# Layer two's up projection, steps one to eight: four quarters over the whole depth become seven half-block products

## The reference, cut to what matters

```python
D_MODEL, SEQ, D_FF, CONV_W = 1024, 512, 2816, 3

def conv_ffn(h, w_up, conv_w, conv_b, w_down):
    S = h.shape[1]
    u = h @ w_up                                  # [512, 1024] @ [1024, 5632]
    up = jnp.pad(u, ((0, 0), (CONV_W - 1, 0), (0, 0)))
    u = conv_b + sum(conv_w[j] * up[:, j:j + S] for j in range(CONV_W))
    gate, val = jnp.split(u, 2, axis=-1)
    return (jax.nn.silu(gate) * val) @ w_down

for layer in range(2):
    x = x + mixer(rms_norm(x, norm_mix[layer]))
    x = x + conv_ffn(rms_norm(x, norm_ffn[layer]), f_w_up[layer], ...)
```

## Time and profile before

| | us |
|---|---|
| median of 3 runs | 1189.49 |
| lowest, highest | 1187.22, 1190.43 |
| the profiled execution, whole | 1190.18 |
| its span | 1188.4 |
| PE busy | 1174.7 (99%) |
| DVE busy | 865.1 (73%) |
| ACT busy | 616.4 (52%) |
| POOL busy | 353.1 (30%) |
| DMA queues' share: SP's, POOL's | 31.2%, 16.3% |
| TensorE's mean granted clock | 0.998 |

### The profile page before, as it was taken

How to read it: one execution, slowest core, us unless ns; L and a number is a source line. 1 busy time by engine, 2 the same in 40 slices (tenths; PEclk the granted TensorE clock), 3 DMA queues, 4 the chain that set the end, 5 groups by cost and what they waited for, 6 DMA issues and landing times.

```text
span 1188.4 us, 18961 instructions
## 1 busy us (share of the span) xinstructions
PE 1174.7 (99%) x6874; PEld 999.3 (84%) x6874; DVE 865.1 (73%) x1502; ACT 616.4 (52%) x1033; POOL 353.1 (30%) x429
## 2 busy tenths in 40 slices
PE   9999999999999999999999999999999999999998
PEld 7768886778888888889999887988888888889998
DVE  6588968945766666579897888855766666579986
ACT  6554337854534333345566789945534334345563
POOL 0633547830042432211000367730042421211000
PEclk9999999999999999999999999999999999999999
DMA  7555352253398785436544110053377574325553
GB/s 277 185 183 204 142 198 69 73 142 106 106 232 243 197 211 194 173 111 212 186 160 138 62 37 2 1 125 107 106 190 182 150 177 132 106 71 196 188 173 127
DMA packets 51555, 174.54 MB, mean 147 GB/s; under 512 B 4720, under 2 KB 6128, under 8 KB 41504
## 3 DMA queue, kind: packets, MB, share of 16 engines
q1 hardware_dynamic: 36352, 127.51, 31.2%
q0 software_dynamic: 15136, 46.14, 16.3%
HBM read 171.50 MB, written 52.47 MB: 188 GB/s over the span
## 4 chain that ended last, share of the span: by engine, by line
PE 92%; DVE 4%; ACT 1%; DMA 1%; issue 1%; POOL 0%; SPq 0%; DVEq 0%; ACTq 0%
PE ps L2558 27%; PE ps L2560 27%; PE ps L2559 27%; PE ps L2273 3%; PE ps L2257 3%; PE ps L2073 1%; PE ps L2524 1%; DMA raw<-w_sums 1%; PE ps L2114 1%; DVE w_lo L1705 1%; PE ps L2144 1%; PE ps L2241 1%; ACT probs L977 1%; DVE xT L1725 0%; PE ps L2081 0%
## 5 line engine op out<-in xcount | busy, mean ns | idle before, releaser
L2558 PE MATMUL ps<-h_hi,w_hi 128*128 128x512 f32 x704 | 274.5, 390 | 0.0
L2560 PE MATMUL ps<-h_hi,w_lo 128*128 128x512 f32 x704 | 273.9, 389 | 0.0
L2559 PE MATMUL ps<-h_lo,w_hi 128*128 128x512 f32 x704 | 273.9, 389 | 0.0
L1394 DVE TENSOR_TENSOR w_lo<-raw,w_hi 128x2048 fp32r<-128x2048 f32 (+1 forms) x62 | 123.0, 1984 | 118.3 <-ACT w_hi L887 118.3
L1216 ACT ACTIVATE cv<-u_in,vec 128x512 f32<-128x512 f32 x88 | 71.2, 816 | 178.8 <-DVE u_in L1835 176.7
L887 ACT ACTIVATE w_hi<-raw 128x2048 fp32r<-128x2048 f32 (+1 forms) x72 | 121.8, 1692 | 69.1 <-PE ps L2560 69.1
L2558 PEld LDWEIGHTS ps<-h_hi,w_hi 128*128 128x128 f32 x704 | 132.2, 188 | 27.8 <-issue 0.7
L2560 PEld LDWEIGHTS ps<-h_hi,w_lo 128*128 128x128 f32 x704 | 132.2, 188 | 27.5
L2559 PEld LDWEIGHTS ps<-h_lo,w_hi 128*128 128x128 f32 x704 | 132.2, 188 | 27.3
L762 POOL TENSOR_TENSOR v<-act 128x256 f32<-128x256 f32 x16 | 43.3, 2709 | 345.2 <-DVE act L1876 345.2
L2558 PE MATMUL ps<-a_hi,w_hi 128*128 128x256 f32 (+1 forms) x440 | 139.0, 316 | 0.8 <-DVE a_lo L1709 0.8
(11 more groups left out here) (276 smaller groups left out, 2426.6 us busy)
## 6 DMA issues: line engine op xcount, KB each, us to landing
raw<-in_f_up SPq DMA_DIRECT2D x44, 1024.0 KB, 5.0
w_sums<-in_f_w_down POOLq DMA_DIRECT2D x22, 1024.0 KB, 8.7
w_sums<-in_f_w_down POOLq DMA_DIRECT2D x44, 512.0 KB, 8.8
raw<-w_sums SPq DMA_DIRECT2D x44, 512.0 KB, 4.1
raw<-in_a_in_wide SPq DMA_DIRECT2D x12, 1024.0 KB, 6.1
raw<-in_f_w_down SPq DMA_DIRECT2D x22, 512.0 KB, 3.9
raw<-in_f_w_down SPq DMA_DIRECT2D x22, 256.0 KB, 3.9
bias_tiles<-bias_rows SPq DMA_DIRECT2D x1, 4096.0 KB, 26.2
```

The source lines that it names most:

```text
L1394: dve.tensor_tensor(w_lo[:, s, 0:n], raw[:, s, 0:n], w_hi[:, s, 0:n].bitcast(F32), ALU.subtract)\
L2558: pe.matmul(dst, s_hi, m_hi, start=start, stop=False)
L2559: pe.matmul(dst, s_hi, m_lo, start=False, stop=False)
L2560: return pe.matmul(dst, s_lo, m_hi, start=False, stop=stop)
```

## The change

Layer one stays as it was in what it computes. In layer two's up projection, steps 1 to 8 are computed by seven products: the step's four channel tiles (gate pair, value pair), the depth (features 0 to 511, 512 to 1023) and the tokens (0 to 255, 256 to 511) are each halved. One product is 2 channel tiles x 4 feature tiles x 3 matmuls of 256 columns, 24 matmuls; a step has 168. ACT copies four intermediate PSUM results out (`keep`), DVE combines them. Before step 1 ACT makes eight gained copies of the features, DVE four sums of halves of them, and both split these into high and low.

Weights arrive in quarters of a slot in a ring of four, 512 KB each: seven for a step of seven products, four for a plain one. Three of the seven are sums or copies in `w_two` and `w_more`: SP copies 16 x 1 MB there in layer one's mixer (`copy_up`: eight behind loads of the input projection, eight in attention), POOL accumulates 16 times 512 KB in layer one's up stage (`two_up`), 8 times behind the key tails of layer two (`three_up`), and 8 times in its attention (`four_up`). Layer one's `w_sums` copies move from POOL to SP's queue in layer one's attention (`copy_down`), layer two's from layer one's up stage to POOL in layer two's attention. The sums are now issued one at a time, each behind a product of PE (`behind`). The hardware loops of the up steps are written out.

The diff, cut to its core:

```diff
...
+SEVENS = ((), (1, 2, 3, 4, 5, 6, 7, 8))
...
+            def copy_down(i):
+                sp.dma_start(w_sums[0][2 * i:2 * i + 2], down_v[0][2 * i:2 * i + 2]).then_inc(up_copied, 16)
+            def copy_up(c):
+                z, h = c // 2, c % 2
+                if z >= len(SEVENS[1]):
+                    return
+                src = f_up[1, SEVENS[1][z]]
+                if h:
+                    sp.dma_start(w_more[1][z], src[0]).then_inc(up_copied, 16)
+                else:
+                    sp.dma_start(w_two[1][z].rearrange("p (a n) -> p a n", a=2), src[:, :, 0:D].rearrange("s p n -> p s n"))\
+                      .then_inc(up_copied, 16)
...
+                    if c >= 4:
+                        copy_up(2 * (c - 4) + s)
...
+                    j = 2 * (i - 2) + e
+                    if j < G_PAIRS:
+                        copy_down(j)
+                    if j % 3:
+                        copy_up(8 + j - j // 3 - 1)
...
+                for m, (i, j) in enumerate(UP_UNITS[l]):
+                    r = m % 4
+                    sp.wait_ge(w_lo_done, U_UP[l] + (1 + m // 2 if m < 4 else m - 1))
+                    if i in SEVENS[l]:
+                        z = SEVENS[l].index(i)
+                        if z == 0 and j in (1, 2, 5):
+                            sp.wait_ge(up_sums, sums_made(l, {1: 4, 2: 5, 5: 6}[j]))
+                        src = (f_up[l, i, 0, :, 0:D], w_two[l][z][:, D:2 * D], w_more[l][z][:, 0:D], f_up[l, i, 0, :, D:2 * D],
+                               w_two[l][z][:, 0:D], w_more[l][z][:, D:2 * D], f_up[l, i, 1, :, D:2 * D])[j]
+                    else:
+                        src = f_up[l, i, j // 2, :, (j % 2) * D:(j % 2 + 1) * D]
+                    sp.dma_start(raw4[:, r, :], src).then_inc(f_raw[r], 16)
...
-            copy_weights(0, 0)
...
+            def two_up(z, h):
+                cols = slice(h * D, (h + 1) * D)
+                pool.dma_start(w_two[1][z][:, cols], f_up[1, SEVENS[1][z], 1][:, cols], accum_op=ALU.add)\
+                    .then_inc(up_sums, 16)
+            def three_up(l, z):
+                if z == 0:
+                    pool.wait_ge(up_sums, sums_made(l, 4))
+                pool.dma_start(w_more[l][z][:, 0:D], w_two[l][z][:, D:2 * D], accum_op=ALU.add).then_inc(up_sums, 16)
+            def four_up(l, z):
+                if z == 0:
+                    pool.wait_ge(up_sums, sums_made(l, 5))
+                pool.dma_start(w_more[l][z][:, D:2 * D], w_more[l][z][:, 0:D], accum_op=ALU.add).then_inc(up_sums, 16)
...
-                copy_weights(0, 1 + u - POOL_LO[0])
...
+            def behind(l, i, j):
+                pool.wait_ge(f_done, DONE_AT[l][i] + j + 1)
+            def sums_of_first():
+                for i in range(1, UP_STEPS):
+                    for j in range(4):
+                        behind(0, i - 1, j)
+                        n = 4 * (i - 1) + j
+                        if n < FT:
+                            sum_weights(0, n)
+                        elif n < FT + 2 * len(SEVENS[1]):
+                            two_up((n - FT) // 2, (n - FT) % 2)
+                        if j == 3 and i > 1:
+                            gate_sums(0, i - 2)
+                for i in range(UP_STEPS - 2, G_PAIRS):
+                    gate_sums(0, i)
+            def sums_of_second():
+                for k in range(FT):
+                    behind(1, *UP_UNITS[1][2 * k])
+                    if k in (4, 8, 12):
+                        gate_sums(1, k // 4 - 1)
+                    sum_weights(1, k)
+                for i in range(3, G_PAIRS):
+                    gate_sums(1, i)
...
+                    if w - 2 * T < len(SEVENS[1]):
+                        three_up(1, w - 2 * T)
...
+                if u % 2 == 0 and 2 <= u < 2 + 2 * len(SEVENS[1]):
+                    four_up(1, u // 2 - 1)
+                elif u % 2 and u >= 3:
+                    copy_weights(1, (u - 3) // 2)
...
+            def gained_features(l):
+                gain_at = G_FFN + l * KD
+                for k in range(KD):
+                    sc.activation(gained[:, k, :], xT[:, k, :], ACT.Identity, scale=gain[:, gain_at + k:gain_at + k + 1])\
+                        .then_inc(t_gained, 1)
...
+                def keep(i, j):
+                    x, _, v_bank = seven_banks(l, i)
+                    bank, dst = {0: (x, kept[:, 0].rearrange("p (a n) -> p a n", a=2)),
+                                 1: (v_bank, kept[:, 1].rearrange("p (a n) -> p a n", a=2)),
+                                 2: (x, u_in[:, 0:2, 2 + HS:2 + S]), 4: (x, u_in[:, 2:4, 2 + HS:2 + S])}[j]
+                    z = SEVENS[l].index(i)
+                    sc.wait_ge(f_done, DONE_AT[l][i] + j + 1)
+                    if j < 2 and z:
+                        sc.wait_ge(f_in, IN_AT[l][i - 1] + j + 1)
+                    if j >= 2:
+                        sc.wait_ge(f_t0, 2 * FT * l + 4 * (i - 1) + j)
+                    sc.activation(dst, both(ps[:, bank, :]), ACT.Copy).then_inc(f_snap, 1)
...
+            def sums_of_features(l, part):
+                if part == 0:
+                    dve.wait_ge(t_gained, LANDED + 4)
+                    dve.tensor_tensor(t_raw[0], x11, x12, ALU.subtract).then_inc(t_summed, 1)
+                    dve.wait_ge(t_gained, LANDED + KD)
+                    dve.wait_ge(t_summed, LANDED + 1)
+                    dve.tensor_tensor(x12, x22, x12, ALU.subtract).then_inc(t_summed, 1)
+                else:
+                    dve.wait_ge(t_summed, LANDED + 2)
+                    dve.scalar_tensor_tensor(x11, x12, -1.0, x11, ALU.mult, ALU.subtract).then_inc(t_summed, 1)
+                    dve.wait_ge(t_summed, LANDED + 3)
+                    dve.scalar_tensor_tensor(x21, x11, -1.0, x21, ALU.mult, ALU.subtract).then_inc(t_summed, 1)
...
+                def first_row(i, t):
+                    _, y, v_bank = seven_banks(l, i)
+                    if t == 0:
+                        dve.wait_ge(f_done, DONE_AT[l][i] + 4)
+                        dve.wait_ge(f_snap, LANDED + SNAP_AT[l][i] + 1)
+                        dve.wait_ge(f_t0, 2 * FT * l + 4 * (i - 1) + 2)
+                        dve.tensor_tensor(u_in[:, 0:2, 2:2 + HS], both(kept[:, 0]), both(ps[:, y, :]), ALU.add)\
+                            .then_inc(f_in, 1)
+                    else:
+                        dve.wait_ge(f_done, DONE_AT[l][i] + 6)
+                        dve.wait_ge(f_snap, LANDED + SNAP_AT[l][i] + 3)
+                        x = u_in[:, 0:2, 2 + HS:2 + S]
+                        dve.tensor_tensor(x, x, both(ps[:, v_bank, :]), ALU.add).then_inc(f_in, 1)
+                        dve.wait_ge(f_in, IN_AT[l][i] + 3)
+                        x = u_in[:, 0:2, 2:2 + S]
+                        dve.tensor_tensor(x, x, rbc[:].unsqueeze(1).to_broadcast([P, 2, S]), ALU.mult).then_inc(f_in, 1)
+                def second_row_sum(i):
+                    dve.wait_ge(f_snap, LANDED + SNAP_AT[l][i] + 4)
+                    x = u_in[:, 2:4, 2 + HS:2 + S]
+                    dve.tensor_tensor(x, x, both(kept[:, 1]), ALU.add).then_inc(f_in, 1)
+                def second_row(i):
+                    bank = seven_banks(l, i)[0]
+                    minus = [rbc_minus[:, t * HS:(t + 1) * HS].unsqueeze(1).to_broadcast([P, 2, HS]) for t in range(2)]
+                    dve.wait_ge(f_done, DONE_AT[l][i] + 7)
+                    dve.wait_ge(f_t0, 2 * FT * l + 4 * (i - 1) + 4)
+                    dve.tensor_tensor(u_in[:, 2:4, 2:2 + HS], both(ps[:, bank, :]), minus[0], ALU.mult).then_inc(f_in, 1)
+                    dve.wait_ge(f_in, IN_AT[l][i] + 2)
+                    x = u_in[:, 2:4, 2 + HS:2 + S]
+                    dve.tensor_tensor(x, x, minus[1], ALU.mult).then_inc(f_in, 1)
...
+                def seven_step(i):
+                    m, behind = unit_of(l, i), i - 1 in SEVENS[l] or i == 1
+                    if i - 1 in SEVENS[l]:
+                        second_row(i - 1)
+                        unit_lo(l, m + 3)
+                    if behind and i > 1:
+                        taps(i - 1, (0, 1))
+                    unit_lo(l, m + 4)
+                    if behind:
+                        if i == 1:
+                            taps(0, (0, 1))
+                        else:
+                            taps(i - 1, (2, 3))
+                    unit_lo(l, m + 5)
+                    if i == 1:
+                        taps(0, (2, 3))
+                        sum_lo(l, 3)
+                    first_row(i, 0)
+                    if behind:
+                        gated(i - 1)
+                    unit_lo(l, m + 6)
+                    second_row_sum(i)
+                    unit_lo(l, m + 7)
+                    unit_lo(l, m + 8)
+                    first_row(i, 1)
+                    unit_lo(l, m + 9)
...
+                def seven_step(i):
+                    banks, z = seven_banks(l, i), SEVENS[l].index(i)
```

(25 more changed lines are left out.)

370 lines of the change are left out of this document (264 added, 106 removed).

## The result

The changed kernel takes 1201.91 us (median of 4 runs, 1200.04 to 1203.17), the kernel before 1189.2 us beside it: a ratio of 1.0107, 95% interval [1.0094, 1.0119]. It is 12.7 us slower, where 1187.3 was forecast and the range ended at 1198.0. The profiled execution has a span of 1201.4 us against 1188.4.

A forecast was written before the change was run, and what follows sets the result against it. PE was taken to bound the kernel, busy 1174.7 of 1188.4 us. Matmuls -12.8, beginning +2.0, transfers +1.0, SP's queue +6.6 and POOL +1.0 gave -2.2, a median of 1187.3 us, range 1179.5 to 1198.

The forecast's parts named there:

- SP's queue in attention one: Layer one's attention: tables wait behind copies in SP's queue, the last lands at 242.3, and PE loses 6.6 us.
- the prediction's slope: SP's queue in layer one's attention: each 0.1 us more per copy delays the last table by 1.8 us.
- the sum: -12.8 +2.0 +1.0 +6.6 +1.0 = -2.2 us; within it, 53.1 us of table and copy transfers on SP's queue.
- the copies are dearer: Rival, chance 0.20: copies on SP's queue cost more than 2.53 us; at 3.0 us each the kernel takes 1195.8.
- named signs of being wrong: Tables landing within 4 us, copies taking over 3 us, or up-step loads landing after 8 us.
- The matmuls: Layer two's up steps: seven products of 256-column matmuls at 0.1198 us save 1.60 us a step, -12.8 us for eight.
- The beginning, +2.0: Layer two's up steps 1 and 2: DVE has 30.4 us of work in 26.5 us, costing +2.0 us.
- transfers, +1.0: Layer two's up steps: weight loads beside accumulating transfers nearly fill the DMA engines, +1.0 us, between 0 and 5.
- POOL in attention two: Layer two's attention: issuing 11 copies and 8 accumulating transfers mostly fits POOL's idle time, +1.0 us, between 0 and 4.
- The wait of the first `four_up`: Layer two's attention: it waits until all eight earlier transfers have landed, perhaps 1 us, within POOL's +1.0.

The follow-up runs named there:

- experiment 4: The changed kernel with SP's copies of down weights and of the first up tensor cut into rows of 8 KB instead of 64 KB pieces: 1200.53 us.
- experiment 3: The changed kernel with the twelve tables of pairs 2 to 7 issued on ScalarE's queue, all 19 copies left in place: 1199.87 us.
- experiment 11: The changed kernel with all nineteen copies in attention one at 512 KB instead of 1 MB, the other halves copied by POOL in the input projection: 1180.23 us.
- experiment 1: The changed kernel with eight copies of up weights moved from attention one to POOL's queue in the output projection behind it: 1182.88 us.
- experiment 5: The changed kernel with eight copies of up weights moved from attention one to POOL in the input projection ahead of it: 1180.77 us.
- experiment 6: Experiment 5's kernel, but four of the eight copies stay in attention one on SP's queue, fifteen copies in all: 1191.95 us.
- experiment 8: Experiment 5's kernel without the 22 accumulating transfers of layer two's down weights beside its up steps (result not the reference's): 1179.17 us.
- experiment 9: Experiment 5's kernel with layer two's eleven copies of down weights issued on SP's queue instead of by POOL in attention two: 1179.36 us.
- experiment 10: Experiment 9's kernel with eight accumulating transfers moved beside layer one's down products and eight behind the key tails, none in attention two: 1177.79 us.
- experiment 2: Experiment 1's kernel with the eleven copies of down weights also moved from attention one, to POOL in the input projection: 1185.68 us.

## Why the prediction was wrong, point by point

**SP's queue in attention one: the term that failed.** Foreseen +6.6, measured +20.2. The prediction named the place, the waits and their order; it sized the transfers too short, the copy at 2.53 us above all. The last table was to land at 242.3 and landed by 257.4. From the first issue at 187.23 to that landing are 70.2 us; by the prediction's own terms, without 2.0 fixed and 12 x 0.63 for the tables, 60.6 us are left for 18 copies, **3.4 us each**. Put back into the prediction's slope, 1.8 us for each 0.1 us, this gives the loss again (8.4 x 1.8 = 15 us more than forecast, 1202); that is the same measurement read twice, and no proof.

What the 3.4 us are made of, the engines' time shows. From 187.2 to 255.4 us, 2.0 fixed before the last landing:

```profile
q1 hardware_dynamic: 3406, 23.44, 97.3%
```

That is 66.4 us of engine time, 2.83 us for each MB. The twelve tables and 18 copies ahead of the last landing are 22.0 MB, 62.3 us where the sum had 53.1: **9.2 us**. Part of that is the tables: the kernel before moved 3.67 MB in 20.8% of 55 us, by which a table takes 0.82 us and not 0.63, 2.2 us for twelve. The other 7.0 us leave about 2.9 us for a copy. A further **4.1 us** went to 1.4 MB of the transfers that stand behind the last table, the nineteenth copy and a load of 512 KB: the sixteen engines together had moved nearly all of them before the table had landed whole. That some engines were ahead of others is my reading of it; the rows do not name the engine. The queue rested 1.8 us, 0.8 more than foreseen, and everything began 1.0 us later. Together these are the 15.1 us from 242.3 to 257.4. Why the same copy takes 2.9 us of the engines here and 2.5 in the earlier trace rows, on POOL's queue and with long rests, was not separated into its causes.

So it was the rival "the copies are dearer", which stood at 0.20 and whose example of 3.0 us, as a price from one copy to the next, was too mild. Neither the form of the pieces (experiment 4) nor the queue's order alone (experiment 3) nor the number of transfers (experiment 11) explains the loss; the amount does (experiments 1, 5, 6 and 11).

The sum itself could have warned: 9.7 us of transfers for each pair of 7.8 us was taken as a delay that adds up slowly. Here, where the queue was asked for more than it could give, no cushion was left, and every error in the price counted as often as there were copies, eighteen times. Of the named signs of being wrong, copies of over 3 us, the spacing of 3.4 us met it, the engines' 2.9 us did not; and tables, said to land after up to 15 us, had medians of 11.1 to 14.6 us, and the last took 18.4.

**The matmuls: right.** The pitch stayed 0.12 us; a product of 24 from `act` begins at 966.14 and the next one 2.88 us later:

```profile
966.14 0.28 PE L2971 MATMUL ps<-act_lo,w_hi 128*128 128x256 f32 x1
...
969.02 0.28 PE L2971 MATMUL ps<-h_hi,w_hi 128*128 128x256 f32 x1
```

Seven of them are 20.2 us, as foreseen, and DVE is busy for 160.45 of 167 us, 96%, without setting the pace.

**The beginning, +2.0, and transfers, +1.0: nearly right.** PE waits 4.1 us in the up stage, in the first steps, and from 961 us on not at all; in experiment 5 it was 3.0, which experiment 8 splits into 1.9 and 1.1, much as foreseen. The stage as a whole came to -8.1 us where -9.8 stood in the sum; the waits are 1.1 of that difference, and 0.6 us stay open (0.8 in experiment 5).

**POOL in attention two: right in kind, +2.0 against +1.0.** POOL is at 60.4 of 68 us, 89% where over 90% was named. Experiments 9 and 10 bring the 2.0 us back in two steps, 1.3 with the copies and 0.7 with the accumulating transfers. The wait of the first `four_up`, which the prediction put at perhaps 1 us, is not in the changed kernel's profile; five others have it, of up to 1.1 us, and there the stage takes up to 2.0 us more (experiment 2).

**Not in the sum: -1.5 us in layer two's down products.** Before, DVE waited 1.9 us at the boundary for a transfer of `w_sums` (the waits of DVE, 1070 to 1095 us of the kernel before):

```profile
DVE raw L1695 <- DMA raw<-w_sums: 1.9, 1, 1.9
```

After the change that wait is not in the list for the same place. In 15 us around the first product with g (1075 to 1090, after the change 1089.5 to 1104.5) PE's idle time fell from 1.8 to 0.7 us. The sum had taken this boundary over unchanged; which of the reordered transfers removes the wait was not tried.

All in all the sum without attention one's term stood at -8.8; measured is 13.0 - 20.2 = -7.2, of which +1.1 is the later start. Without the later start that is -8.3, and the closeness to -8.8 is in part luck: the up stage (+1.7) and attention two (+1.0) came out worse than foreseen, and the down products (-1.5) and layer one's feed-forward block (-0.7), for which nothing stood in the sum, better. One term made the forecast wrong in sign.

## What to carry to other kernels

Before work is put on a queue that also carries something an engine waits for, add up the transfer time that one period brings, and compare it with the period, at a price measured on transfers that follow each other without rest; here 75% of the engines' time cost next to nothing and 93% cost 12 us, and a second queue adds no engine time, since the engines behind it are the same. Copies that nobody waits for belong where the engines have room and nothing urgent moves beside them: moving eight of nineteen turned a loss of 1% into a gain of 0.5%, and moving layer two's helpers as well into one of 1%. When a forecast rests on one price times eighteen, put the spread of that price into the likeliest case, not into a rival.
